# Rearranging the bucket steps, one projection tile and the compressed attention branch of a three-layer transformer kernel

## The reference

```python
# first block: one wide projection, cut into parts
z = h @ w_in                       # a_q 512, a_k 64, a_v 64, i_q 256, i_k 64, i_w 4, c_q 256, c_kv 128, k_r 32, gates 2048
# branch a: attention over the keys an index picks, with a bias by distance bucket
bias = rel_table[rel_bucket(posq - take_rows(positions, sel))]     # 32 buckets, 8 heads
# branch b: k_r (32 columns) is the rotary part of the keys

# last layer, "compressed" branch: 15 blocks of 32 tokens at stride 16, 2 key groups of 8 heads
kc = gelu(flat_k @ w1_k) @ w2_k    # flat: [15, 2, 32*64], w1: [2048, 256], w2: [256, 64]
vc = gelu(flat_v @ w1_v) @ w2_v
p_c = softmax(q @ kc + bias(t - c_end), masked to c_end <= t) * c_valid
o = gate0 * (p_c @ vc) + gate1 * o_slc + gate2 * o_win
out = o @ w_o
```

## Time and profile before

| | |
|---|---|
| median of 3 runs | 1033.54 us (1033.35 to 1035.8) |
| profiled execution, its own time | 1040.78 us |
| its span, first to last instruction | 1038.7 us |
| PE busy | 1014.0 us (98%) |
| DVE, ACT, POOL busy | 702.3, 564.5, 203.1 us |
| mean granted TensorE clock | 0.987 |

### The profile page before, as it was taken

The page is one execution under the profiler, slowest core; times in us unless marked ns, Lnnn a source line. Parts: engine busy times, 40 slices in busy tenths (PEclk is TensorE's granted clock), DMA queues, the critical chain, the costliest instruction groups (busy, mean ns, idle before and its releaser), DMA issues.

```text
span 1038.7 us, 23202 instructions
## 1 busy us (share of the span) xinstructions
PE 1014.0 (98%) x8620; PEld 994.2 (96%) x8620; DVE 702.3 (68%) x1377; ACT 564.5 (54%) x1111; POOL 203.1 (20%) x231
## 2 busy tenths in 40 slices
PE   7999999999999999999999999999999999999998
PEld 7999999999999999998999999999989999999997
DVE  6699767777765557887666655586755776667543
ACT  6564674566664436765545454467965555454431
POOL 6000000633434333012111112200000211111230
PEclk9999999999999999999999999999987999999999
DMA  9825424646565558245666567581341366665831
GB/s 279 189 82 160 135 74 130 194 138 198 168 206 194 182 182 205 81 114 139 193 173 191 151 182 212 171 225 32 96 158 42 83 173 190 176 188 141 234 112 41
DMA packets 221506, 161.36 MB, mean 155 GB/s; under 512 B 7379, under 2 KB 214584, under 8 KB 221434
## 3 DMA queue, kind: packets, MB, share of 16 engines
q1 hardware_dynamic: 218746, 154.30, 49.8%
q0 software_dynamic: 2544, 6.04, 3.1%
q10 hardware_dynamic: 144, 0.07, 0.0%
HBM read 158.28 MB, written 2.10 MB: 154 GB/s over the span
## 4 chain that ended last, share of the span: by engine, by line
PE 83%; DVE 7%; ACT 5%; issue 2%; POOL 1%; SPq 0%; DMA 0%; DVEq 0%; ACTq 0%; POOLq 0%
PE bank L640 24%; PE bank L642 23%; PE bank L641 23%; PE bank L919 4%; DVE w_lo L1913 3%; PE bank L907 2%; ACT w_hi L1292 2%; ACT work L1480 1%; PE bank L891 1%; PE bank L892 1%; PE bank L894 1%; ACT big L1494 1%; PE bank L810 1%; PE bank L933 0%; DVE steps L1999 0%
## 5 line engine op out<-in xcount | busy, mean ns | idle before, releaser
L1913 DVE TENSOR_TENSOR w_lo<-raw,w_hi 128x1024 fp32r<-128x1024 f32 (+2 forms) x297 | 361.9, 1225 | 158.8 <-ACT w_hi L1292 156.2
L640 PE MATMUL bank<-hh,w_hi 128*128 128x256 f32 x1384 | 397.0, 287 | 0.8 <-DVE w_lo L1913 0.6
L641 PE MATMUL bank<-hl,w_hi 128*128 128x256 f32 x1384 | 393.2, 284 | 0.0
L642 PE MATMUL bank<-hh,w_lo 128*128 128x256 f32 x1384 | 393.1, 284 | 0.0
L1292 ACT ACTIVATE w_hi<-raw 128x1024 fp32r<-128x1024 f32 (+2 forms) x297 | 301.0, 1033 | 136.3 <-PE bank L642 133.5
L640 PEld LDWEIGHTS bank<-hh,w_hi 128*128 128x128 f32 x1384 | 265.7, 192 | 2.9 <-issue 1.3
L641 PEld LDWEIGHTS bank<-hl,w_hi 128*128 128x128 f32 x1384 | 265.9, 192 | 0.2
L642 PEld LDWEIGHTS bank<-hh,w_lo 128*128 128x128 f32 x1384 | 265.7, 192 | 0.1
L640 PE MATMUL bank<-hidh,w_hi 128*128 128x256 f32 x672 | 189.3, 282 | 1.2 <-POOL hidl L2776 1.2
L641 PE MATMUL bank<-hidl,w_hi 128*128 128x256 f32 x672 | 188.9, 281 | 0.0
L642 PE MATMUL bank<-hidh,w_lo 128*128 128x256 f32 x672 | 188.9, 281 | 0.0
(11 more groups left out here) (304 smaller groups left out, 1245.1 us busy)
## 6 DMA issues: line engine op xcount, KB each, us to landing
raw<-ffn_w_gu_in SPq DMA_DIRECT2D x88, 512.0 KB, 4.9
raw<-w_ff_in SPq DMA_DIRECT2D x64, 512.0 KB, 4.2
raw<-w_in_in SPq DMA_DIRECT2D x26, 512.0 KB, 5.1
raw<-ffn_w_down_in SPq DMA_DIRECT2D x32, 384.0 KB, 4.2
raw<-ffn_w_down_in SPq DMA_DIRECT2D x32, 320.0 KB, 3.4
raw<-b_w_in_in SPq DMA_DIRECT2D x14, 512.0 KB, 7.1
raw<-a_w_qkv_in SPq DMA_DIRECT2D x10, 512.0 KB, 4.9
raw<-w_out_in SPq DMA_DIRECT2D x8, 512.0 KB, 4.5
```

The source lines that it names most:

```text
L640: pe.matmul(o, ah, bh, start=start, stop=False)
L641: pe.matmul(o, ah, bl, start=False, stop=False)
L642: return pe.matmul(o, al, bh, start=False, stop=stop)
L1913: dve.tensor_tensor(tile_view(w_lo, n), raw_view(n), tile_view(w_hi, n).bitcast(F32), ALU.subtract)\
```

## The change

In the first block:

- The slot of `w_in` behind the first holds 224 columns from `i_q` on and the 32 columns of `k_r`. Tile n+3 so has 128 columns and the tile of `k_r` is gone; everything behind `c_kv` has a number one lower. ACT copies `k_r` out of the same bank; the transposes of `i_w` and `k_r` on PE stand together, and so do DVE's copies. DVE computes the rotary angles (L2125 to L2142) before it waits for them.
- Key `128*(c//2) + 32*i + 16*(c%2) + g` lies in partition block `i` of call `c`. Tile `t=0` needs calls 0 and 1 alone, with 128 partitions; tile `t=1` needs four. `step_sums(2, (0,))` and `step_sums(3, (0,))` are gone with their `key_steps` and `bias_sums`. Each remaining call of `t=0` has twice the partitions and 32 instead of 16 columns. `key_steps(3, (1,))` stands ahead of `take_largest(0, 5, 8)`.

In the last layer:

- The compressor's input holds the high and the low part side by side (`xc`, 60 columns) as one stationary operand: two products for each chunk instead of three; the two halves of the result are summed by a matmul with two stacked identities (`fold`, made once by POOL), where before a transpose was.
- `compressor_rows` runs on POOL.
- Units 16 to 19 are gone. In their place, for each group: 16 score matmuls of 30 columns into one bank (keys' high and low part side by side), `compressed_soften` and `compressed_normal` on DVE over all heads and both tiles at once (240 elements a partition) with one `exp` on ACT between, one transpose for each tile of 8 heads by 15 keys (`compressed_turn`), and values laid out as a block diagonal (120 rows) by DVE, so that `compressed_columns` gives columns directly.
- The sum over the branches is made in PSUM: `branch_columns` multiplies the rows of the other branches by the identity (plain matmuls) into the bank to which `compressed_columns` adds. ACT and DVE then write `yh` and `yl`, two banks for each group. The gate of the compressed branch and the mask of its first 31 rows are applied to the probabilities.

The core of the diff:

```diff
-    plain("w_in", 0, 0, KC, IN_AK + 256, 256)
+    slot(KC, 256, [("w_in", 0, 0, KC, IN_AK + 256, 224, 0, 0), ("w_in", 0, 0, KC, IN_KR, MR, 0, 224)], [(0, P), (P, P)])
     plain("w_in", 0, 0, KC, IN_CQ, 256)
-    plain("w_in", 0, 0, KC, IN_CKV, 160)
+    plain("w_in", 0, 0, KC, IN_CKV, P)
...
-                    rows, width = (64, 16) if t == 0 else (P, 32)
-                    pe.wait_ge(steps_d, 2 * c + t + 1)
+                    pe.wait_ge(steps_d, STEPS[c, t])
                     b = STEP_BANK[t]
-                    open_bank(b, (b1_ev, 2 * c + t + 1))
+                    open_bank(b, (b1_ev, STEPS[c, t]))
                     for g in range(16):
-                        o = psum[b][:, width * g:width * g + width]
+                        o = psum[b][:, 32 * g:32 * g + 32]
                         for i in range(3):
-                            mm = pe.matmul(o, steps[t][0:rows, g, :], rhs4p[i][0:rows, 0:width // 8, :],
-                                           start=(i == 0), stop=(i == 2))
+                            mm = pe.matmul(o, steps[t][:, g, :], rhs4p[i][:, :, :], start=(i == 0), stop=(i == 2))
...
-            tile_ready(n + 7)
-            open_bank(1, ev["krT"])
-            feature_tile(n + 7, half(1)[0:MR, :], hh, hl).then_inc(tiles_done, 1)
...
-                if j == 1:
-                    step_sums(2, (0,))
...
-                if j == 4:
-                    step_sums(3, (0,))
...
-            key_steps(2)
+            key_steps(2, (1,))
...
+            key_steps(3, (1,))
+            prefetch(n + 17)
             take_largest(0, 5, 8)
-            prefetch(n + 17)
             take_largest(1, 0, 2)
-            key_steps(3)
...
-                            at = slice(2 * NC * jp, 2 * NC * (jp + 1))
-                            mm = mm3(half(0)[0:2 * NC, :], xch[:, kv, at], xcl[:, kv, at],
-                                     wh[:, k, :], wl[:, k, :], jp == 0, jp == 15)
+                            pair = xc[:, kv, jp, :, :].rearrange("p l c -> p (l c)")
+                            pe.matmul(half(0)[0:4 * NC, :], pair, wh[:, k, :], start=(jp == 0), stop=False)
+                            mm = pe.matmul(half(0)[0:4 * NC, :], pair, wl[:, k, :], start=False, stop=(jp == 15))
...
+                    def compressed_scores(g, t):
+
+                        if t == 0:
+                            open_bank(S_BANK, (c_seen, g + 1))
+                        for h in range(HU):
+                            at = 2 * NC * (HU * t + h)
+                            mm = pe.matmul(psum[S_BANK][:, at:at + 2 * NC], qs[:, HU * g + h, P * t:P * t + P],
+                                           ck2[:, g, :, :], start=True, stop=True)
...
+                    def compressed_turn(g):
+
+                        pe.wait_ge(c_ready, g + 1)
+                        open_bank(0, (c_turned, g + 1))
+                        for t in range(NT):
+                            mm = pe.transpose(psum[0][0:C_ROWS, P * t:P * t + P], c_prob[:, g, HU * t:HU * t + HU, :]
+                                              .rearrange("p h k -> p (h k)"), ident[:, :])
...
+                    def branch_columns(g, b):
+
+                        bank = C_COLUMNS[g][b]
+                        open_bank(bank, (y_done, 9 + 2 * g + b))
+                        for c in range(2):
+                            for t in range(NT):
+                                pe.wait_ge(acc_done, 2 * g + t + 1)
+                                at = T * c + P * t
+                                heads = slice(4 * b + 2 * c, 4 * b + 2 * c + 2)
+                                pe.matmul(psum[bank][:, at:at + P], y_acc[g][t][:, heads, :].rearrange("p a b -> p (a b)"),
+                                          ident[:, :], start=(c == 0 and t == 0), stop=False)
+
+                    def compressed_columns(g):
+
+                        pe.wait_ge(*ev["cv"])
+                        pe.wait_ge(c_turned, g + 1)
+                        for b, bank in enumerate(C_COLUMNS[g]):
+                            for c in range(2):
+                                heads = slice(4 * b + 2 * c, 4 * b + 2 * c + 2)
+                                mm = pe.matmul(half(bank, c), c_vals[0:C_ROWS, g, heads, :].rearrange("p a b -> p (a b)"),
+                                               c_turn[0:C_ROWS, g, :, :].rearrange("p t q -> p (t q)"), start=False, stop=(c == 1))
+                            close_bank(mm, f"cY{g}{b}", bank)
...
+                    branch_columns(0, 0)
...
+                    pe.wait_ge(*ev["ck"])
+                    compressed_scores(0, 0)
+                    branch_columns(0, 1)
+                    compressed_scores(0, 1)
                     values(15)
-                    pe.wait_ge(*ev["ck"])
-                    scores(16)
-                    scores(17)
-
-                    transposes(16, (0, 1))
-                    scores(18)
-                    transposes(16, (2, 3))
-                    pe.wait_ge(*ev["cv"])
-                    values(16)
-                    transposes(17, (0, 1))
-                    scores(19)
-                    transposes(17, (2, 3))
-                    values(17)
-                    rows_to_columns(16)
-                    transposes(18, (0, 1))
-                    transposes(18, (2, 3))
-                    rows_to_columns(17)
-                    values(18)
-                    first_half(0, 2)
-                    transposes(19, (0, 1))
+                    compressed_turn(0)
+                    compressed_scores(1, 0)
+                    compressed_columns(0)
+                    compressed_scores(1, 1)
+                    branch_columns(1, 0)
+                    branch_columns(1, 1)
+                    first_half(0, 1)
...
+                    compressed_turn(1)
+                    first_half(2, 2)
+                    compressed_columns(1)
+                    for fc in range(3, 8):
+                        first_half(fc, (1, 3, 2)[fc % 3])
...
+                    def compressed_soften(g):
+                        dve.wait_ge(*filled[f"cS{g}"])
+                        src = psum[S_BANK][:, 0:4 * NC * HU * NT // 2].rearrange("p (n l k) -> p n l k", l=2, k=NC)
+                        s = c_prob[:, g, :, :]
+                        step(dve.tensor_tensor(s, src[:, :, 0, :], biasC[:, g, :, :, :].rearrange("p t h k -> p (t h) k"), ALU.add))
+                        settled()
+                        dve.tensor_tensor(s, src[:, :, 1, :], s, ALU.add).then_inc(c_seen, 1)
+                        dve.wait_ge(c_seen, g + 1)
+                        step(dve.tensor_reduce(c_max[:, g, :], s, AX.X, ALU.max))
+                        settled()
+                        dve.tensor_tensor(s, s, c_max[:, g, :].unsqueeze(2).broadcast_to([P, NT * HU, NC]), ALU.subtract)\
+                           .then_inc(c_shift, 1)
+
+                    def compressed_normal(g):
+                        s, total = c_prob[:, g, :, :], c_sum[:, g, :]
+                        dve.wait_ge(c_exp, g + 1)
+                        step(dve.tensor_reduce(total, s, AX.X, ALU.add))
+                        settled()
+                        step(dve.reciprocal(total, total))
+                        settled()
+                        by_tile = total.rearrange("p (t h) -> p t h", t=NT)
+                        step(dve.tensor_tensor(by_tile, by_tile, gate48[:, :, 24 * g:24 * g + 22:3], ALU.mult))
+                        settled()
+                        dve.tensor_tensor(s, s, total.unsqueeze(2).broadcast_to([P, NT * HU, NC]), ALU.mult).then_inc(c_ready, 1)
...
+                    compressed_soften(0)
+                    prefetch(ST["wo1"] + 2)
+                    compressed_normal(0)
+                    prefetch(ST["wo1"] + 3)
+                    compressed_low(0)
+                    compressed_soften(1)
+                    compressed_normal(1)
+                    add_half(0, 1)
+                    add_half(2, 2)
+                    compressed_low(1)
+                    for fc in range(3, 8):
+                        add_half(fc, (1, 3, 2)[fc % 3])
...
+            def compressor_rows(name, kv):
+
+                pool.wait_ge(*sc[name])
+                for g in range(2):
+                    for a in range(2):
+                        src = scaled_at(name)[HD * g:HD * g + HD, a:a + 1]
+                        src = bass.AP(tensor=src.tensor, offset=src.offset, ap=[src.ap[0], [2, 16], [16, NC]])
+                        dst = xc_raw[HD * a:HD * a + HD, kv, :].rearrange("p (j g c) -> p j g c", j=16, g=2)
+                        ins = pool.tensor_copy(dst[:, :, g, :], src)
```

More of the change, by code:

```diff
@@ L1185, in _ @@
                     transposes(13, (2, 3))
+                    compressor(5)
                     scores(15)
+                    compressor(6)
+                    compressor(7)
                     values(13)
-                    for i in range(5, 8):
-                        compressor(i)
```

(36 more changed lines are left out.)

333 lines of the change are left out of this document (157 added, 176 removed).

## The result

The changed kernel takes **1008.62 us** (median of four runs, 1006.06 to 1010.38) against 1033.61 of the kernel before in the same session: a ratio of 0.9751, 95% interval 0.9729 to 0.9773. Forecast were 1009.5 us and a range of 1003 to 1017. The profiled execution took 1009.19 us, its span is 1007.4 us.

What follows compares the result with a forecast made beforehand. PE was taken as the bound, with DVE the other bound in the first block. 7.0 us there plus 17 in the last layer (13.1 + 5.2 - 1.5) made 24, so 1033.5 - 24 = 1009.5 us, range 1003 to 1017.

Steps and rivals of the forecast that it cites:

- First block: 7.0 forecast: First block: DVE's gain sets the end, PE's surplus turns into waits; 7.0 us less, between 4.5 and 7.9.
- The walk of DVE: First block, DVE in its new order: index score begins at 45.7 us, `neg_ready` falls at 101.4 instead of 108.8.
- DVE without a gap longer than 1 us from 46 us: First block, a sign to look for: DVE runs on from 46 us with no gap above 1 us.
- The net: Last layer, PE work at full clock: 24.1 us removed, 11.0 us added, 13.1 us less.
- the forecast's 1.5 us lost to waits: Last layer, PE's waits: 4.5 us against 3 before, so 1.5 us lost.
- So I keep one stretch: 5.2 us come back of 10.3: Last layer, PE's clock: one of two half-clock stretches stays, around `ck`, `cv` and the first 30-column scores; 5.2 us gained.
- the first rival: Last layer: the clock stays up, no stretch at half clock; 5 us more gain, 1004.5 us; chance 0.20.
- The median is 7.2 us below this execution; the same difference gives 1033.5 - 24: Whole kernel: the 24 us taken off the profiled execution also come off the median, giving 1009.5 us.
- The clock falling twice: Last layer: clock falls twice, or group 1's chain isn't covered; 5 us less gain, 1014.5, both 1017.5; chance 0.22.
- Slower by POOL's copies: Last layer: POOL's strided copies delay the second compressor half, from 6.0 us a copy eating the 24 us; chance 0.05.
- The angles given back: First block: DVE gives back the angles, so the gain there is 4.5 us, time 1012 us; chance 0.10.
- the work not saved: Last layer: small matmuls cost as much as those they replace; gain 8 instead of 17, 1018.5 us; chance 0.03.

Runs made afterwards that it cites:

- the repeated profile of before: The kernel before, unchanged, run and profiled once more: 1033.36 us, ratio 1.0001; its profile took 1033.84 us with a clock of 0.993.
- angles_back: The changed kernel with the rotary angles computed at their old place, right ahead of the index scores on DVE: 1011.32 us, ratio 0.9782.
- scores_twice: The changed kernel with each of the 32 score products of 30 columns issued twice: 1019.13 us, ratio 0.9858.
- no_cover: The changed kernel with group 0's eight branch_columns products moved from among the short products to behind values(15): 1013.23 us, ratio 0.9810.
- tile_ahead: The changed kernel with compressor(5) on PE ahead of transposes(13, (2, 3)) instead of behind: 1006.24 us, ratio 0.9742.
- no_cover_again: The kernel of no_cover, unchanged, once more for more runs and a second profile: 1012.75 us, ratio 0.9791.
- the changed kernel in its repeated profile: The changed kernel, unchanged, run again beside three others on the same chip: 1009.0 us, ratio 0.9746.

## Why the prediction was right

The forecast was right to 1 us of the median, and in part by luck: the first block came out as said, in the last layer two errors cancelled.

**First block: 7.0 forecast, 6.1 by the runs, 6.5 and 6.9 by the two profiles of before.** The mechanism was right: DVE sets the end, and what PE saved beyond that turned into waits. Removed on PE: the `k_r` tile, the step sums and the fall at 84 to 92 us, as said. The waits came out as 0.57 for a gate tile, 1.44 for the next and 0.88 for `neg_ready`, 2.9 us in place of 4.4; those for `w_ukv` don't exist. The walk of DVE was 0.8 us early: the index score began at 46.48, not 45.7, since ACT's high part of that tile came later than assumed (the 44.20 that the walk took for its start is the start of DVE's low part in the trace of before; the high part was ready at 44.10 there and holds DVE up to 45.34 here), and the wait for step sum (1,1) was 1.47 and not 0.6; the release fell at 102.3 instead of 101.4. DVE in the changed kernel:

```profile
45.34 1.23 DVE L1916 TENSOR_TENSOR w_lo<-raw,w_hi 128x1024 fp32r<-128x1024 f32 x1 [4.36 <-ACT w_hi L1317]
46.48 0.35 DVE L2114 SCALAR_TENSOR_TENSOR work<-work,iw,causal 128x128 f32<-128x128 f32 x1
...
63.05 2.29 DVE L2001 TENSOR_TENSOR steps<-pos_f,thrG 128x2048 bf16<-128x2048 f32 x1 [1.47 <-PE bank L814]
```

"DVE without a gap longer than 1 us from 46 us" was therefore wrong in one place. The angles were hidden, as forecast: 1.8 of their 2.1 us.

**Last layer, work.** PE's timeline of the changed kernel around the new products:

```profile
759.03 1.06 PE L1191 MATMUL bank<-ident_sb,work 128*128 128x128 f32 x8
760.01 0.42 PE L1244 MATMUL bank<-work,cw 128*64 128x30 f32 x4
760.36 1.05 PE L1250 MATMUL bank<-cw,ompressed_hidden_by_head 128*120 128x64 f32 x8
761.25 1.04 PE L901 MATMUL bank<-ident_sb,work 128*128 128x128 f32 x8
762.30 1.06 PE L1168 MATMUL bank<-compressed_keys,qs 128*128 128x30 f32 x8
763.21 1.14 PE L1191 MATMUL bank<-ident_sb,work 128*128 128x128 f32 x8
764.11 1.04 PE L1168 MATMUL bank<-compressed_keys,qs 128*128 128x30 f32 x8
765.00 3.76 PE L913 MATMUL bank<-work,big 128*128 128x64 f32 x32
...
769.92 1.97 PE L1201 MATMUL bank<-sed_probabilities_turned,compressed_values 120*128 120x256 f32 x8
771.54 1.15 PE L1168 MATMUL bank<-compressed_keys,qs 128*128 128x30 f32 x8
```

The 30-column scores take 0.11 us (8 in 0.91), 3.6 us in all against 3.5. Of the two rules of the Trainium skill (TensorE: Matmul & The Clock Gate), the load of 128 stationary columns (LDWEIGHTS) fits, the floor for few moving columns (Back-to-back issue gap) doesn't. `branch_columns` take 0.115 a row of the trace and not 0.105, 3.7 us against 3.4; `compressed_columns` 0.20, 3.2 against 3.4. The folding products (L1232, 8 rows in 1.0 us where 4 took 0.3) were missing from the sum. Added 11.8 in place of 11.0. The net is still as forecast: PE's busy time in the last layer's part goes from 70.97 us, less 3.4 for the clock (the repeated profile of before), to 54.54, so 13.0 against 13.1, and what went must be worth some 24.8 instead of 24.1.

**Last layer, waits.** Before `transposes(13, (2, 3))` 1.33 (1.4 said), before the last compressor tile 0.40 (0.7 said). The 0.6, 0.4 and 0.4 around `ck`, `cv` and the scores don't exist: PE comes to `ck` at 760.01, and DVE's gelu is done at 759.5. So the forecast's 1.5 us lost to waits became 0.7 us gained: in that part PE is idle for 2.56 us in the repeated profile of before (73.53 - 70.97) and for 1.82 in the changed kernel's (56.36 - 54.54).

**Last layer, clock: the step that failed.** "So I keep one stretch: 5.2 us come back of 10.3" was wrong on both sides. The trace of the changed kernel has no stretch, so the first rival (given 0.20) is what happened: the part forecast at 62 us takes 56.4, and beside the first profile of before the gain is 31.3 us and not 24. The rival's 1004.5 us didn't come, because the 10.3 us weren't there to be won back. "The median is 7.2 us below this execution; the same difference gives 1033.5 - 24" carried the profile's clock loss over into a median that has a quarter to a third of it (2.7 us by the runs, 3.4 in the repeated profile).

That repeated profile (1033.84 us) is an ordinary execution, so the median's gain can be read from it and the changed kernel's. The spans differ by 1032.1 - 1007.4 = 24.7 us:

| | forecast | measured |
|---|---|---|
| up to the first transpose that waits for `neg_ready` | 7.0 | 6.9 (109.18 to 102.33) |
| from there to the first compressor tile | in the next row | 2.0 (630.9 to 628.8) |
| from there to the last addition of `first_half`, without the clock | 11.6 | 13.8 (75.1 less 3.4, to 58.0) |
| its clock | 5.2 | 3.4 |
| behind it | 0 | -1.4 (216.9 to 218.3) |

In the third row 13.0 are work and 0.7 waits, where 13.1 and -1.5 were forecast: beside the clock it was the waits that were mis-sized, by 2.2 us. By the first profile of before the row is 12.6 (22.9 less 10.3), so it is known to 1 us or so. Of the 2.0 a wait of 0.56 us for ACT at 733.50 us, which is gone, is one part; the rest, and the 1.4 behind, aren't traced to a cause. So the sum was right because 4.2 us too little for work and waits stood against 1.8 too much for the clock and 1.4 given back that the sum didn't have.

**The other rivals.** The clock falling twice: no run. Slower by POOL's copies: all eight together, the view of their line in the changed kernel (durations are ns, least, median, most):

```profile
L2820 POOL COPY work<-work x8: 589/600/1055, 713.1 to 719.4; 64x240 f32<-64x240 f32 x8
```

0.60 us in place of 1.0, a tenth of the 6.0 that would have hurt. The angles given back and the work not saved: out, by `angles_back` and the stretches.

## What to carry to other kernels

Before a profile's difference is taken for the median's, look where its own time lies among the runs: here the profiled execution was slower than 62 others, and 10 of its us were lost to a half clock of which the median has a quarter to a third. Products that can stand anywhere are best tried among the short ones and their waits: here 1.7 us of them were worth 4 by their place. A change that only adds short products can cost more than twice their own time: here 3.6 us of them cost 10. Where a saved product turns into a wait, find the engine that releases it and move its work behind the release: here two selection rounds were worth 2.1 us of the trace.

## What the runs showed of the chip

- The granted clock of PE fell from 2.4 to 1.2 GHz after 32 products of 30 moving columns, with four of 128 (eight rows of the trace) between them and no wait (`scores_twice`: 0.56 over 764 to 778 us). The busy share of the profile doesn't show it: PE is busy for 14.00 of these 14 us. The Trainium skill (TensorE: Matmul & The Clock Gate, The HAM clock gate) says that activity releases the throttle. The trace here doesn't bear that out as far as it can show it: PE had been busy without a gap from 749.86 us on when the clock fell, near 766.
- The same kernel falls in some runs and not in others: by their mean clock eight of ten runs of `no_cover` had a fall in the last layer, and none of nine of the changed kernel. Of the two `no_cover` profiles, one has the fall and one doesn't.
- All profiles, of both kernels, have one more stretch at a lower clock at 32 to 40 us, worth 1.7 to 3.4 us, which none of these edits touches; that of `tile_ahead` has another before 30 us (0.94 over the first 30). It isn't in every run: one run of the changed kernel has a mean clock of 1.00 and takes 1005.82 us.
- Two profiles, `no_cover_again` and `scores_twice`, take 57.3 us for a stretch of the last feed-forward part (from PE's wait of 0.56 us for POOL to its wait for the last variance) that takes 59.3 to 60.0 in the other twelve, with the same instructions and a granted clock of 1.00 in all: 179 products in 20 us against 172. They are the two that had a fall in the changed kernel's last layer, and it gives 2.2 us of its cost back. What links the two stays open.

```profile
950.00:970.00 20.00, 20.00 (x179) 20.00 (x179) 9.40 (x8) 7.98 (x6) 6.44 (x6) 1.00 0.68 195
```

```profile
945.00:965.00 20.00, 20.00 (x172) 20.00 (x171) 9.40 (x8) 7.47 (x6) 5.63 (x5) 1.00 0.66 186
```

The first is `no_cover_again`, the second the changed kernel in its repeated profile, 20 us from about the same place of the work.
